# RMS factors applied after the first products, and the residual transposed and split by token tiles during the last output panel

## What is computed

```python
def rms_norm(x, g):
    y = x * lax.rsqrt(jnp.mean(x * x, axis=-1, keepdims=True) + EPS)
    return y * g

def first_block(x, ...):
    for layer in range(DEPTH):                      # DEPTH = 2
        h = rms_norm(x, mix_norm[layer])
        mixed = rglru_mixer(h, ...) if layer == 0 else fox_mixer(h, ...)
        x = x + mixed
        x = x + sq_relu_mlp(rms_norm(x, mlp_norm[layer]), mlp_w1[layer], mlp_w2[layer])
    return x

def sq_relu_mlp(h, w1, w2):
    return jnp.square(jax.nn.relu(h @ w1)) @ w2     # 1024 -> 4096 -> 1024

def fox_mixer(h, w_in, b_f, q_gain, k_gain, w_out): # 16 heads of 64
    q, k, v, f_logit = jnp.split(h @ w_in, [D, 2 * D, 3 * D], axis=-1)
    q, k = rms_norm(heads(q), q_gain), rms_norm(heads(k), k_gain)
    c = jnp.cumsum(jax.nn.log_sigmoid(f_logit + b_f), axis=1)
    ...                                             # causal softmax with c, times v
    return o @ w_out
```

## Time and profile before

| what | value |
|---|---|
| median of 3 runs | 1954.89 us (1953.85 to 1954.91) |
| the profiled execution: its own time, its span | 1950.85 us, 1949.7 us |
| PE busy | 1785.9 us (92%) |
| DVE, ACT, POOL busy | 712.5, 518.6, 54.9 us |
| mean granted TensorE clock | 0.969 |
| HBM traffic | 275 GB/s over the span; about 428 GB/s in the expert stage |

### The profile page before, as it was taken

How to read it: one execution, slowest core, us unless ns; L and a number is a source line. 1 busy time by engine, 2 the same in 40 slices (tenths; PEclk the granted TensorE clock), 3 DMA queues, 4 the chain that set the end, 5 groups by cost and what they waited for, 6 DMA issues and landing times.

```text
span 1949.7 us, 23208 instructions
## 1 busy us (share of the span) xinstructions
PE 1785.9 (92%) x8779; PEld 1009.9 (52%) x8780; DVE 712.5 (37%) x1050; ACT 518.6 (27%) x694; POOL 54.9 (3%) x67
## 2 busy tenths in 40 slices
PE   7989997987999999998699999999999998999996
PEld 6769996776899877554433333332333322333332
DVE  3544445653544403552323222222222222222323
ACT  1445543543554403321011111111111111111111
POOL 0000001000000010220000000000000000000000
PEclk9989998988999999998799999999999999999998
DMA  7344553421454532330599999999999997899995
GB/s 256 134 162 173 190 199 97 173 78 43 144 202 173 178 112 104 130 130 0 216 378 429 428 430 428 428 429 428 429 429 428 429 428 305 359 429 428 428 430 224
DMA packets 84958, 537.02 MB, mean 275 GB/s; under 512 B 8736, under 2 KB 8840, under 8 KB 60328
## 3 DMA queue, kind: packets, MB, share of 16 engines
q1 hardware_dynamic: 79088, 531.64, 67.3%
q10 hardware_dynamic: 5816, 4.59, 0.8%
HBM read 535.17 MB, written 1.05 MB: 275 GB/s over the span
## 4 chain that ended last, share of the span: by engine, by line
PE 66%; DMA 24%; DVE 5%; ACT 2%; issue 1%; ACTq 0%; POOL 0%; SPq 0%; PEldq 0%; DVEq 0%; POOLq 0%
DMA expert_ring<-in_expert_w_up 23%; PE psA L1677 19%; PE psA L483 10%; PE psB L461 9%; PE psB L367 6%; PE psA L389 4%; PE psB L472 3%; PE psA L1179 2%; PE psB L376 2%; PE psA L1683 1%; PE psB L808 1%; PE psB L351 1%; PE psB L1706 1%; PE psB L1186 1%; PE psA L743 1%
## 5 line engine op out<-in xcount | busy, mean ns | idle before, releaser
L1677 PE MATMUL psA<-expert_ring,gathered_T 128*64 128x512 f32 x1024 | 454.7, 596 | 30.7 <-DMA expert_ring<-in_expert_w_up 30.7
L1678 PE MATMUL psA<-expert_ring,gathered_T 128*64 128x512 f32 x1024 | 454.7, 596 | 0.0
L1677 PEld LDWEIGHTS psA<-expert_ring,gathered_T 128*64 128x64 f32 x1024 | 134.9, 137 | 343.1 <-issue 280.8
L442 DVE TENSOR_TENSOR w_low<-panel_ring,w_high 128x1024 fp32r<-128x1024 f32 x160 | 194.6, 1225 | 167.2 <-ACT w_high L435 167.1
L1677 PE MATMUL psA<-expert_ring,activated_T 128*64 128x512 f32 x528 | 240.5, 598 | 3.2 <-ACT activated_T L1938 0.9
L1678 PE MATMUL psA<-expert_ring,activated_T 128*64 128x512 f32 x528 | 240.5, 598 | 0.0
L435 ACT ACTIVATE w_high<-panel_ring 128x1024 fp32r<-128x1024 f32 x160 | 168.1, 1057 | 197.2 <-PE psB L461 96.9
L2068 DVE TENSOR_SCALAR normed<-psA 128x512 f32<-128x512 f32 x32 | 22.1, 692 | 396.0 <-PE psA L1678 396.0
L1897 ACT ACTIVATE normed<-normed 128x512 f32<-128x512 f32 x32 | 20.2, 631 | 473.6 <-DVE normed L2068 473.6
L461 PE MATMUL psB<-hT_high,w_high 128*128 128x256 f32 x512 | 145.6, 284 | 0.0
L461 PE MATMUL psB<-hT_high,w_low 128*128 128x256 f32 x512 | 144.9, 283 | 0.0
(11 more groups left out here) (425 smaller groups left out, 2412.8 us busy)
## 6 DMA issues: line engine op xcount, KB each, us to landing
expert_ring<-in_expert_w_up SPq DMA_DIRECT2D x128, 2048.0 KB, 25.4
expert_ring<-in_expert_w_down SPq DMA_DIRECT2D x64, 2048.0 KB, 22.3
panel_ring<-in_mlp_w SPq DMA_DIRECT2D x32, 2048.0 KB, 8.1
panel_ring<-in_w_in SPq DMA_DIRECT2D x11, 2048.0 KB, 8.0
panel_ring<-in_fox_w_in SPq DMA_DIRECT2D x6, 2048.0 KB, 8.0
panel_ring<-in_lru_w_in SPq DMA_DIRECT2D x4, 2048.0 KB, 17.0
panel_ring<-in_lru_w_out SPq DMA_DIRECT2D x2, 2048.0 KB, 8.0
panel_ring<-in_fox_w_out SPq DMA_DIRECT2D x2, 2048.0 KB, 7.9
```

Of the source, the lines that this page charges most:

```text
L442: V.tensor_tensor(w[1], view, w[0].bitcast(F32), ALU.subtract).then_inc(s.w_low, 1)
L1677: M.matmul(ps[0:SLOTS], lhsT, rhs[0], **flags)
L1678: return M.matmul(ps[SLOTS:P], lhsT, rhs[1], **flags)
```

## The change

1. The squares of `x` still run on ACT (`squares_act`), but after the split of the input; the factor is not applied to `x`. `x` itself is transposed and times the gain becomes `hT`.
2. In the MLPs the factor comes in as its square, 1 / (mean square + EPS), when `psA` is added to `x` (`scalar_tensor_tensor` with `rms_stats[:, 4]`). `x` is no longer multiplied into `psA`.
3. In Fox, v is scaled when it is evicted (two ACT instructions in place of one for each of its two panels); q and k use the squared factor in their own mean square and the factor in their scale; the logits are multiplied by r, spread over columns by two more products, on two added DVE instructions.
4. The last output panel of each MLP and of Fox runs all its parts for token tile 0 and then all for tile 1 (`product_out_last`). After the first part of tile 1 (in Griffin: after its first chunk) PE transposes tile 0 of the updated `x`. DVE and ACT update, scale and split tile 0 while PE goes on with tile 1, and split the next layer's parts between these steps (`turn_dve`, `turn_act`).
5. The first two parts of each MLP (`product_T_tile`) and the four parts of Fox's first panel run by token tiles: tile 0 of all of them, then tile 1. For the MLP parts a product then has 128 moving columns in place of 256, and there are 96 in place of 48; Fox keeps its 512 columns and its number.

```diff
-def rms_act(k, r):
-    A, s, st, xn = k.nc.scalar, k.s, k.rms_stats, xn_of(k)
-    for g, tiles in enumerate(GROUPS[r]):
-        for tt in tiles:
-            A.wait_ge(*x_ready(k, r, tt))
-            A.activation(xn[:, tt, :], k.x[:, tt, :], ACT.Square, accum_out=st[:, 0, tt:tt + 1]).then_inc(s.squared, 1)
-        at = slice(tiles[0], tiles[-1] + 1)
-        A.wait_ge(s.variance, GROUP_OF[r] + g + 1)
-        A.activation(st[:, 2, at], st[:, 1, at], ACT.Sqrt).then_inc(s.rooted, 1)
...
+def squares_act(k, r):
+    A, s, st = k.nc.scalar, k.s, k.rms_stats
+    for tt in range(TT):
+        A.wait_ge(*x_ready(k, r, tt))
+        A.activation(k.xn[:, tt, :], k.x[:, tt, :], ACT.Square, accum_out=st[:, 0, tt:tt + 1]).then_inc(s.squared, 1)
...
-def rms_dve(k, r, gain):
...
-        for tt in tiles:
-            V.wait_ge(*x_ready(k, r, tt))
-            V.tensor_scalar(xn[:, tt, :], k.x[:, tt, :], st[:, 2, tt:tt + 1], None, ALU.mult).then_inc(s.normed, 1)
...
+def mean_square_dve(k, r):
+    V, s, st = k.nc.vector, k.s, k.rms_stats
+    V.wait_ge(s.squared, 2 * r + 2)
+    V.tensor_scalar(st[:, 1], st[:, 0], 1.0 / D, EPS, ALU.mult, ALU.add).then_inc(s.variance, 1)
+    V.wait_ge(s.variance, r + 1)
+    V.reciprocal(st[:, 4], st[:, 1]).then_inc(*k.dve.step())
...
+def rows_T_pe(k, r, tt, source, ready):
+    M = k.nc.tensor
+    M.wait_ge(*ready)
+    for c in range(KD):
+        last = M.transpose(by_tile(k, tt)[:, c, :], source[:, tt, c * P:(c + 1) * P], k.ident[:])
+    last.then_inc(k.s.x_T, 1)
+def x_T_pe(k, r, tt):
+    rows_T_pe(k, r, tt, k.x, x_ready(k, r, tt))
+def hT_dve(k, r, tt, gain):
+    V, s = k.nc.vector, k.s
+    to = k.hT[:, :, tt * P:(tt + 1) * P]
+    V.wait_ge(s.x_T, 2 * r + tt + 1)
+    if gain is None:
+        V.tensor_copy(to, by_tile(k, tt)).then_inc(s.hT_ready, 1)
+    else:
+        V.tensor_tensor(to, by_tile(k, tt), gain.unsqueeze(2).to_broadcast([P, KD, P]), ALU.mult).then_inc(s.hT_ready, 1)
...
+def accumulate_nat(k, p, aT, first, last, between=None):
...
+        if between and (c, tt) == (0, 1):
+            between()
     mm.then_inc(s.consumed, 1)
...
+def x_updates_dve(k, first, done, scale=None):
     V, s = k.nc.vector, k.s
-    for tt in range(TT):
+    def update(tt):
         if tt == 0:
             V.wait_ge(s.out_first, first)
         else:
             V.wait_ge(*done)
-        V.tensor_tensor(k.x[:, tt, :], k.x[:, tt, :], flat(k.psA[:, 2 * tt:2 * tt + 2, :]), ALU.add).then_inc(s.x_updated, 1)
+        x, products = k.x[:, tt, :], flat(k.psA[:, 2 * tt:2 * tt + 2, :])
+        if scale is None:
+            V.tensor_tensor(x, x, products, ALU.add).then_inc(s.x_updated, 1)
+        else:
+            V.scalar_tensor_tensor(x, products, scale[:, tt:tt + 1], x, ALU.mult, ALU.add).then_inc(s.x_updated, 1)
+    return update
...
+def product_T_tile(k, p, i, out, tt):
+    h, w = h_parts(k), [v[:].rearrange("p (k n) -> p k n", n=P) for v in split_part(k, p, i)]
+    cols = slice(tt * P, (tt + 1) * P)
+    for c in range(KD):
+        for a, b in PARTS:
+            last = k.nc.tensor.matmul(out[:, cols], w[a][:, c, :], h[b][:, c, cols], start=(c == 0 and a == b),
+                                      stop=(c == KD - 1 and a == 1))
+    if tt == TT - 1:
+        last.then_inc(k.s.part_done, 1)
...
+def product_out_last(k, p, a_parts_of, between):
+    s, w = k.s, []
+    for tt in range(TT):
+        for i in range(4):
+            if tt == 0:
+                w.append(split_part(k, p, i))
+            last = out_tile(k, w[i], a_parts_of(i), tt, False, i == 3)
+            if tt == TT - 1:
+                last.then_inc(s.part_done, 1)
+                if i == 0:
+                    between()
+        if tt == 0:
             last.then_inc(s.out_first, 1)
-    last.then_inc(s.part_done, 1)
...
+def turn_act(k, r, following):
+    p, kind = following
+    high(k, p, 0, kind)
+    high_h(k, r - 1, 0)
+    high(k, p, 1, kind)
+    high(k, p, 2, kind)
+    high(k, p, 3, kind)
+    high_h(k, r - 1, 1)
+    squares_act(k, r)
+def turn_dve(k, r, gain, update, following):
+    p, kind = following
+    update(0)
+    hT_dve(k, r, 0, gain)
+    low(k, p, 0, kind)
+    low_h(k, r - 1, 0)
+    update(1)
+    low(k, p, 1, kind)
+    hT_dve(k, r, 1, gain)
+    low(k, p, 2, kind)
+    low_h(k, r - 1, 1)
+    low(k, p, 3, kind)
...
 def mlp_dve(k, layer, t):
...
-    V.wait_ge(s.part_done, mlp_part_done(layer, 63))
-    for tt in range(TT):
-        V.tensor_copy(k.x[:, tt, :], flat(k.psA[:, 2 * tt:2 * tt + 2, :])).then_inc(s.x_updated, 1)
+    V.wait_ge(*k.dve.last())
+    done = (s.part_done, mlp_part_done(layer, 63))
+    update = x_updates_dve(k, OUT[f"mlp{layer}"], done, k.rms_stats[:, 4])
+    if layer == 0:
+        turn_dve(k, 2, k.col("mix", KD, KD), update, (FOX, BY_TWO_ROWS))
+    else:
+        for tt in range(TT):
+            update(tt)
+            hT_dve(k, 4, tt, None)
...
 def mlp_pe(k, layer, t):
...
-    M.wait_ge(s.x_updated, 4 * layer + 2)
-    for tt in range(TT):
-        for half in range(2):
-            M.matmul(k.psA[:, 2 * tt + half, :], k.ident[:], k.x[:, tt, half * 512:(half + 1) * 512], start=True, stop=False)
-    M.wait_ge(s.h_low, TT * (2 * layer + 1))
+    n, p = 2 * layer, MLP[layer]
+    up = lambda j, i: by_four(k.psB[j])[:, i, :]
+    x_T_pe(k, n + 1, 1)
+    M.wait_ge(s.h_low, TT * n + 1)
+    product_T_tile(k, p, 0, up(0, 0), 0)
+    product_T_tile(k, p, 1, up(0, 1), 0)
+    M.wait_ge(s.h_low, TT * n + 2)
+    product_T_tile(k, p, 0, up(0, 0), 1)
+    product_T_tile(k, p, 1, up(0, 1), 1)
...
+            if (trip, j) == (3, 1):
+                M.wait_ge(s.u_read, 8 * layer + 8)
+                product_out_last(k, p + 3, row, lambda: x_T_pe(k, 2 * layer + 2, 0))
...
 def fox_pe(k, f):
...
-    M.wait_ge(s.h_low, TT * 2)
-    for j in range(4):
+    M.wait_ge(s.h_low, TT + 1)
+    product_nat(k, FOX, 0, k.psB[0], [0])
+    x_T_pe(k, 2, 1)
+    for i in range(1, 4):
+        product_nat(k, FOX, i, k.psB[0], [0])
+    M.wait_ge(s.h_low, TT + 2)
+    for i in range(4):
+        product_nat(k, FOX, i, k.psB[0], [1])
+    for j in range(1, 4):
         project(j)
     M.wait_ge(s.late, 96)
     M.wait_ge(s.x_updated, 4)
     for c in range(KD):
         last = M.matmul(k.psA[0:NH, 0, 0:T], f.wf[:, c, :], k.hT[:, c, :], start=(c == 0), stop=(c == KD - 1))
+    M.wait_ge(s.r_spread, 2)
+    for tt in range(TT):
+        last = M.matmul(k.psA[0:NH, 1, tt * P:(tt + 1) * P], k.ones[:, 0:NH], f.r_diag[:, tt, :], start=True, stop=True)
     last.then_inc(s.f_products, 1)
     for j in (4, 5):
         project(j)
...
 def fox_act(k, f):
...
+            A.wait_ge(s.r_spread, 2)
+            for tt in range(TT):
+                last = A.activation(to[:, tt, :], k.psB[j % 2][:, tt, :], ACT.Copy, scale=k.rms_stats[:, 2, tt:tt + 1])
...
 def fox_dve(k, f):
...
+    mean_square_dve(k, 2)
+    root_dve(k, 2)
+    V.wait_ge(*dve.last())
+    V.tensor_scalar(f.r2[:], k.rms_stats[:, 4], 1.0 / HD, None, ALU.mult).then_inc(*dve.step())
+    for tt in range(TT):
+        V.tensor_scalar(f.r_diag[:, tt, :], k.ident[:], k.rms_stats[:, 2, tt:tt + 1], None, ALU.mult).then_inc(s.r_spread, 1)
...
+    V.wait_ge(s.f_products, 1)
+    V.tensor_copy(f.lf[:, 1, :], k.psA[0:NH, 0, 0:T]).then_inc(*dve.step())
+    V.wait_ge(*dve.last())
+    V.tensor_tensor(f.lf[:, 1, :], f.lf[:, 1, :], k.psA[0:NH, 1, 0:T], ALU.mult).then_inc(s.f_scaled, 1)
...
+    heads = lambda i, tt: f.ss[:, i, :, tt * NH:(tt + 1) * NH]
+    for tt in range(TT):
+        V.tensor_scalar(heads(0, tt), heads(0, tt), f.r2[:, tt:tt + 1], EPS, ALU.mult, ALU.add).then_inc(s.qk_var, 1)
...
+    for tt in range(TT):
+        V.tensor_scalar(heads(1, tt), heads(1, tt), k.rms_stats[:, 2, tt:tt + 1], None, ALU.mult).then_inc(*dve.step())
+    V.wait_ge(*dve.last())
```

210 lines of the change are left out of this document (104 added, 106 removed).

## The result

| | before | changed |
|---|---|---|
| median | 1954.37 us (1950.51 to 1954.91, 4 runs) | 1916.42 us (1915.64 to 1917.94, 4 runs) |
| ratio, 95% interval | | 0.9815 (0.9802 to 0.9827) |
| profiled execution, span | 1950.85, 1949.7 us | 1916.36, 1915.2 us |

The page of the changed kernel: the line of busy time and the chain of waits by engine; it answers to the earlier trace rows.

What follows compares the result with a forecast made beforehand. TensorE was busy 92% of the span, with the winnable time in the four turns between layers. 8.3 + 13.9 + 10.7 + 4.4 - 2.0 = 35.3 us off 1950.85 gave 1915.6, or 1919.6 for the median; range 1912 to 1942.

Steps and rivals of the forecast that it cites:

- Price of the narrow product: First two parts of each MLP: a 128-column product costs 0.111 us, one weight load, so 96 take 10.7 us.
- Rivals 1, 2 and 4: Narrow products at turns A and C: 0.22 us each (1940.9, chance 0.20); under weight load (1911.5, 0.15); 0.43 (1980.8, 0.02).
- Turn A: Griffin's last panel into MLP 0: the first two parts end at 122.35 instead of 130.6, gain 8.3 us.
- Turn B: MLP 0's last panel into Fox: Fox's first panel is done at 319.6 instead of 333.5, gain 13.9 us.
- Turn C: Fox's last panel into MLP 1: parts 0 and 1 are done at 491.35 instead of 502.1, gain 10.7 us.
- Turn D: MLP 1's end into the hybrid: hybrid starts at 680.5 instead of 683.0, at full clock, gain 4.4 us.
- Fox pays back 2.0: Fox after the q and k products: added r products, DVE instructions and scalings cost 2.0 us, bounds 0.5 and 3.
- Rival 3: TensorE's clock falls in the turns, each losing about 1.9 us: 1927.2; chance 0.10.
- Rival 5: No change: the expert stage, which the DMA bounds, absorbs the gain: 1954.9; chance 0.03.

Runs made afterwards that it cites:

- 64 columns: Changed kernel with each narrow product cut into two of 64 columns, 192 at a turn instead of 96; 1979.57 us, ratio to before 1.0144.
- part 19 early: Changed kernel with the split of Fox's fourth v part moved ahead of the log f chain and head norms; 1917.40 us, ratio to before 0.9810.
- whole products: Changed kernel with the first two parts of each MLP whole again, 48 products of 256 columns; 1916.74 us, ratio to before 0.9818.
- one narrow: Changed kernel with only the first part of each MLP by token tiles, the second whole; 1921.95 us, ratio to before 0.9839.
- row order: Changed kernel with the last panels of MLP 0, Fox and MLP 1 part by part again, both tiles in each; 1941.42 us, ratio to before 0.9942.

## Why the prediction was right

By its own steps:

- **Price of the narrow product, 0.111 us.** Measured 0.111 (10.67 / 96), and 0.111 again with 64 columns. The nearer row, f32 products of 64 columns, was the right guide. Rivals 1, 2 and 4 fall by it.
- **Turn A, 8.3.** 8.50. **Turn B, 13.9.** 13.79, with the two short waits for `w_low` in the chain. **Turn C, 10.7.** 10.73. **Turn D, 4.4.** 4.03; the two hybrid panels behind it took 27.89 us, not 2 x 13.81. That the clock held at D was partly luck (below).
- **Fox pays back 2.0.** From the start of the logits to the fourth v part the changed kernel takes 359.34 - 345.33 = 14.01 us, and the kernel before 12.03 by the same two points: 1.98, as forecast. The whole stage lost only 1.33, since eight transposes behind it took 1.08 us in place of 1.96, which was not foreseen, and the eviction of v 0.24 more, where the forecast had 0.1. The run with part 19 early removed this wait by an edit of its own, so it is shown that the splitting of that part behind the head norms was what TensorE waited for. The edit moved ACT's half as well; that DVE's half came last is read from the chain (358.06).
- **Rival 3, the clock falls in the turns.** It did not fall in any of the four, in the profiled execution. At D it is right in part: of nine kernels with the code of D as changed, the clock fell there in four, for 1.7 to 3.1 us. The Trainium skill ("TensorE: Matmul & The Clock Gate", section "Part 4: PE-mode transpose") says that transposes do not count as work that keeps the clock up, and this rival had its chance from that. Here the measurement decides against it: 5.46 us of nothing but transposes left the clock at 1.00, and transposes put in a wait kept it up at A and at C in all three kernels that had them, where it had fallen at A and C in all three without them.
- **Rival 5, no change.** The part from the hybrid on took 1236.9 us against 1237.2. The expert stage absorbed nothing of the gain.

The forecast for the median, 1919.6, was 3.2 us above the 1916.4 measured, inside the range; for the profiled execution it was 0.8 below it (1915.6 against 1916.36). The step that was off is the last one, from the profile to the median: the profiled execution of before lay 4.0 us under its median, and the prediction added these 4.0; that of the changed kernel lay 0.1 under its own, and the runs of before that were made later have medians of 1951 to 1952 us. The start (1.5 us lost) and the stage behind the turns (0.3 won) lie outside the sum; the stages that the change touches gained 35.7 us, with 35.3 forecast.

What the prediction did not see is how near the edge it was. It took the narrow products for 4.9 us more work at a turn, to be paid for by the early start. The experiments show what they buy: without them the clock falls (whole products), with half of them it falls (one narrow), with idle time ahead of them they are run at half clock (row order), and with half their columns they lose it themselves. Each turn came out within 0.4 us because the clock held, so that every price read at full clock was the right one. At A and C the change happens to leave no gap behind the transposes; at D it leaves 1.3 us, and there the same code lost the clock in other kernels.

One thing stays open. Where the clock falls outside the turns (Fox's attention and output products, turn D, the hybrid's output panels, the router) differs between runs whose code there is the same, by 2 to 3 us at a place. It isn't settled what sets it. Of the changed kernel and the twelve made from it, six had the router's products in 4.6 to 4.7 us, and in all six the expert stage took 983.0 to 984.3 us; in the seven with 7.05 us it took 978.9 to 981.4. So what is won at the router is given back, and the traces show where. In the changed kernel and then in the one before, the same eight records of TensorE behind the router (chain of waits):

```profile
943.68 3.78 PE psB L1890 x4
947.46 2.87 PE psA L1890 x4
```

```profile
982.13 1.98 PE psB L1743 x4
984.12 1.72 PE psA L1743 x4
```

In the changed kernel the clock comes back to 1.00 at 949.6 us, 18.5 us behind the router's products, and in the one before at 979.8, 9.6 us behind them. That costs the first products of the expert stage 3.5 us, in all six kernels alike. Why the clock comes back later stays open.
